# A hybrid decoder step on one core: another order for the opening's copies, table load, small loads and transposes

## The reference

```
h = rmsnorm(x, norm1_g);  z = h @ w_in             # 2824 columns
u, x_rg, g_rg, q, k, v, o, gi, gf = split(z)
y1, s5 state  = s5_mixer(u, ...)                   # diagonal complex state space model
y2, rg state  = rglru_mixer(x_rg, g_rg, ...)       # causal conv, two gates, recurrence
y3, ml state  = mlstm_mixer(q, k, v, gi, gf, o, ...)
x = x + concat(y1, y2, y3) @ w_out
x = x + moe(rmsnorm(x, norm2_g), ...)              # top 4 of 32 experts, clamped SwiGLU
y = rmsnorm(x, final_norm_g)

# s5_mixer, before its scan, from parameters alone:
step = exp(log_step); mag = exp(lam_re * step)
ab   = mag * (cos(lam_im * step) + i sin(lam_im * step))
z    = (ab - 1) / lam;   bb = z * b
```

## Time and profile before

| | |
|---|---|
| three runs | 1098.27, 1098.32, 1098.80 us; median 1098.32 |
| the profiled execution's own time | 1098.81 us |
| its span, first to last instruction | 1097.0 us (1.8 us lie around it) |
| PE busy | 1036.5 us, 94% |
| DVE, ACT, POOL busy | 316.1, 197.9, 95.3 us |
| HBM traffic over the span | 390 GB/s |
| mean granted TensorE clock | 0.993 |

### The profile page before, as it was taken

The page is one execution under the profiler, slowest core; times in us unless marked ns, Lnnn a source line. Parts: engine busy times, 40 slices in busy tenths (PEclk is TensorE's granted clock), DMA queues, the critical chain, the costliest instruction groups (busy, mean ns, idle before and its releaser), DMA issues.

```text
span 1097.0 us, 13183 instructions
## 1 busy us (share of the span) xinstructions
PE 1036.5 (94%) x5134; PEld 435.2 (40%) x5134; DVE 316.1 (29%) x640; ACT 197.9 (18%) x418; POOL 95.3 (9%) x177
## 2 busy tenths in 40 slices
PE   8999999999999999899889989999899989998997
PEld 5767745334333433343333323333324233433322
DVE  5889456312131212121202112121212121212023
ACT  5543615401110201011000201020102010100002
POOL 6899000000000000000000000000000000000000
PEclk9999999999999999999999999999999999999999
DMA  7533799999999999999999999999999999999995
GB/s 223 194 114 77 260 370 406 427 426 431 430 433 430 430 431 431 431 431 431 434 431 431 431 431 431 431 431 434 431 430 431 431 431 431 431 433 431 424 426 239
DMA packets 62051, 429.45 MB, mean 391 GB/s; under 512 B 12022, under 2 KB 25054, under 8 KB 33342
## 3 DMA queue, kind: packets, MB, share of 16 engines
q1 hardware_dynamic: 60868, 428.16, 93.5%
q10 hardware_dynamic: 1146, 0.79, 0.2%
HBM read 424.68 MB, written 3.67 MB: 390 GB/s over the span
## 4 chain that ended last, share of the span: by engine, by line
PE 55%; DMA 36%; DVE 5%; ACT 2%; issue 1%; SPq 1%; ACTq 0%; DVEq 0%
DMA ring_a<-in_exp_w_dram 27%; PE psum L2405 17%; PE psum L2440 14%; DMA ring_b<-in_exp_w_dram 8%; PE psum L2426 7%; PE psum L2327 3%; PE psum L2158 3%; PE psum L2350 2%; PE psum L1886 2%; PE psum L2449 1%; PE psum L2277 1%; PE psum L2283 1%; DVE rgb L1341 1%; SPq L449 1%; DMA xn<-in_x_prompt_dram 1%
## 5 line engine op out<-in xcount | busy, mean ns | idle before, releaser
L2405 PE MATMUL psum<-ring_a,xg 128*64 128x512 f32 x1200 | 341.8, 600 | 14.4 <-DMA ring_a<-in_exp_w_dram 14.4
L2440 PE MATMUL psum<-ring_a,aT 128*64 128x512 f32 x768 | 217.7, 596 | 8.5 <-DMA ring_a<-in_exp_w_dram 8.2
L2405 PEld LDWEIGHTS psum<-ring_a,xg 128*64 128x64 f32 x1200 | 102.9, 137 | 170.1 <-issue 166.0
L2405 PE MATMUL psum<-ring_b,xg 128*64 128x512 f32 x368 | 152.3, 598 | 7.8 <-DMA ring_a<-in_exp_w_dram 7.8
L1672 DVE TENSOR_TENSOR x<-x,psum 128x512 f32<-128x512 f32 x60 | 41.2, 687 | 367.7 <-PE psum L2350 367.7
L2426 PE MATMUL psum<-ring_a,xg 128*64 128x512 f32 x336 | 103.5, 608 | 14.2 <-DMA ring_b<-in_exp_w_dram 14.2
L2440 PEld LDWEIGHTS psum<-ring_a,aT 128*64 128x64 f32 x768 | 68.0, 137 | 110.2 <-issue 104.3
L2440 PE MATMUL psum<-ring_b,aT 128*64 128x512 f32 x256 | 104.0, 595 | 4.2 <-DMA ring_a<-in_exp_w_dram 2.6
L1760 DVE TENSOR_SCALAR acts<-psum 128x512 f32<-128x512 f32 x32 | 22.0, 688 | 223.3 <-PE psum L2426 207.8
L1045 ACT ACTIVATE acts<-acts 128x512 f32<-128x512 f32 x32 | 20.1, 627 | 296.5 <-DVE acts L1760 296.5
L2405 PEld LDWEIGHTS psum<-ring_b,xg 128*64 128x64 f32 x368 | 43.1, 136 | 75.5 <-issue 63.6
(11 more groups left out here) (508 smaller groups left out, 934.9 us busy)
## 6 DMA issues: line engine op xcount, KB each, us to landing
ring_a<-in_exp_w_dram SPq DMA_DIRECT2D x144, 2048.0 KB, 26.3
ring_b<-in_exp_w_dram SPq DMA_DIRECT2D x46, 2048.0 KB, 24.8
ring_a<-in_w_in_dram SPq DMA_DIRECT2D x4, 2048.0 KB, 8.5
ring_a<-in_w_out_dram SPq DMA_DIRECT2D x2, 2048.0 KB, 9.8
ring_a<-in_w_in_dram SPq DMA_DIRECT2D x3, 1024.0 KB, 5.9
ring_a<-in_state_ml_c_dram SPq DMA_DIRECT2D x4, 512.0 KB, 6.1
out_dram<-ring_a SPq DMA_DIRECT2D x4, 512.0 KB, 6.1
ring_b<-in_exp_w_dram SPq DMA_DIRECT2D x2, 1024.0 KB, 28.5
```

What stands on the lines that cost most here:

```text
L2405: m = M(psum[64 * x:64 * x + 64, bk, :], xg[:, k, u, 64 * x:64 * x + 64], w[x][:, 512 * bk:512 * bk + 512], start=False, stop=(k == KD - 1))
L2440: m = M(psum[64 * x:64 * x + 64, 4 + nn, :], aT[:, 2 * j + s, 64 * x:64 * x + 64], w[x][:, 1024 * s + 512 * nn:1024 * s + 512 * nn + 512], ...
```

## The change

1. VectorE copies five halves, in the order hT0, hT2, hT4, hT3, hT5; ScalarE copies only hT1.
2. TensorE's one wait for six copies is split: three left halves before u0, three right halves behind u0's fourth step. Of three warming matmuls between and behind the transposes one is left, behind the last.
3. `mag` waits for its own semaphore `mag_arg`, which L1252 raises (VectorE no longer waits for itself there), and ScalarE's wait for `angle_reduced` moves to just ahead of the first Sin, behind the other three functions.
4. On SyncE the five loads of the states' rows go ahead of the gate columns; `glw` goes behind w_in's second slab.
5. The `par` transposes move from between u1 and gp to behind the sixth step of xr0.
6. ScalarE's order of copies becomes u0, u1, gp, `bias_piece(0)`, par (was u0, `bias_piece(0)`, u1, par, gp).

```diff
 SyncE, if c == 1:
+                    for x, name in enumerate(("state_s5_re", "state_s5_im")):
+                        sp.dma_start(srow[64 * x:64 * x + 64, :], ...).then_inc(sem("par_loaded"), 16)
+                    sp.dma_start(prow[0:32, :], ...)       # state_ml_n
+                    sp.dma_start(prow[32:48, :], ...)      # state_rg_h
+                    sp.dma_start(prow[48:96, :], ...)      # state_rg_conv
                     sp.wait_ge(sem("wgate_zero"), 1)
                     sp.dma_start(wgate[:, :, 0:2 * H], w_in_cols(GI0, 2 * H)).then_inc(sem("wgate_loaded"), 16)
...
-                    (the same five loads)
                     sp.dma_start(gb[:], ...)
                     sp.dma_start(m0[:], ...)
+                if c == 2:
                     sp.dma_start(glw[:], ...)
-                if c == 2:
                     sp.wait_ge(*at("weights_zero", 1))
 ScalarE:
-            for i in range(2):
-                name = f"hT{2 * i + 1}"
-                await_fill(act, name)
-                for c in range(4):
-                    m = A(hT[:, 4 + c, 128 * i:128 * i + 128], bank(name)[...], ACT.Copy, scale=vec("norm1_g", 4 + c))
+            await_fill(act, "hT1")
+            for c in range(4):
+                m = A(hT[:, 4 + c, 0:128], bank("hT1")[...], ACT.Copy, scale=vec("norm1_g", 4 + c))
...
             A(sm[:, 1, :], vecs[:, NVEC:NVEC + J5], ACT.Exp).then_inc(says_now("step_ready"), 1)
-            act.wait_ge(*at("angle_reduced", 1))
+            act.wait_ge(sem("mag_arg"), 1)
             A(sm[:, 5, :], sm[:, 2, :], ACT.Exp).then_inc(says_now("mag_ready"), 1)
             A(rsm[:, 0:2], vec("rg_lambda"), ACT.Abs).then_inc(says_now("act_rg"), 1)
             act.wait_ge(*at("act_rg", 1))
             A(g_exp[:, 12:14], rsm[:, 0:2], ACT.Exp, scale=-1.0).then_inc(says_now("act_rg"), 1)
+            act.wait_ge(*at("angle_reduced", 1))
             A(sm[:, 6, :], sm[:, 9, :], ACT.Sin).then_inc(says_now("angle_ready"), 1)
...
             u_out(0)
+            u_out(1)
+            copy_out("gp", gate_parts, bank("gp")[:, 0:T])
             bias_piece(0)
-            u_out(1)
             copy_out("par", parT[:, 0:224], bank("par")[:, 0:224])
-            copy_out("gp", gate_parts, bank("gp")[:, 0:T])
 VectorE:
-            for k in (0, 2, 4, 5):
+            for k in (0, 2, 4, 3, 5):
...
-            dv(TT(sm[:, 2, :], lr, sm[:, 1, :], ALU.mult))
+            TT(sm[:, 2, :], lr, sm[:, 1, :], ALU.mult).then_inc(sem("mag_arg"), 1)
 TensorE:
             for k in range(2, 6):
                 turn_half(k)
-                if k == 3:
-                    keep_warm(1)
-            keep_warm(2)
-            for k in range(6):
-                b, f = FILLS[f"hT{k}"]
-                pe.wait_ge(drained[b], f + 1)
+            keep_warm(1)
+            def rows_turned(hf):
+                for i in range(len(TILES)):
+                    b, f = FILLS[f"hT{2 * i + hf}"]
+                    pe.wait_ge(drained[b], f + 1)
...
+            def state_rows(k):
+                if k == 5:
+                    pe.wait_ge(sem("par_loaded"), 16 * 5)
+                    await_bank(pe, "par")
+                    TR(bank("par")[:, 0:128], srow[:], ident[:])
+                    ends_fill(TR(bank("par")[:, 128:224], prow[0:96, :], ident[0:96, 0:96]), "par")
+            rows_turned(0)
             pe.wait_ge(sem("w_in0"), 16)
-            channels("u0", 0, 0)
+            channels("u0", 0, 0, lambda k: rows_turned(1) if k == 3 else None)
             channels("u1", 0, 128)
-            (the wait for par_loaded and the two transposes)
             pe.wait_ge(sem("wgate_loaded"), 16)
             gate_products()
             pe.wait_ge(sem("w_in0_right"), 16)
-            channels("xr0", 0, 256)
+            channels("xr0", 0, 256, state_rows)
```

More of the change, by code:

```diff
@@ L469, in _ @@
                 if c == 1:
+                    for x, name in enumerate(("state_s5_re", "state_s5_im")):
+                        sp.dma_start(srow[64 * x:64 * x + 64, :], a[name][0].rearrange("b (j g) p -> (b j) (g p)", g=2)).then_inc(sem("par_loaded"), 16)
+                    sp.dma_start(prow[0:32, :], a["state_ml_n"][0].rearrange("b h k -> (b h) k")).then_inc(sem("par_loaded"), 16)
+                    sp.dma_start(prow[32:48, :], a["state_rg_h"][0].rearrange("b (x n) -> (b x) n", x=2)).then_inc(sem("par_loaded"), 16)
+                    sp.dma_start(prow[48:96, :], a["state_rg_conv"][0].rearrange("b t (x n) -> (b t x) n", x=2)).then_inc(sem("par_loaded"), 16)
                     sp.wait_ge(sem("wgate_zero"), 1)
@@ L738, in _ @@
             act.wait_ge(drained[FILLS["vec"][0]], 1)
-            for i in range(2):
-                name = f"hT{2 * i + 1}"
-                await_fill(act, name)
-                for c in range(4):
-                    m = A(hT[:, 4 + c, 128 * i:128 * i + 128], bank(name)[:, 128 * c:128 * c + 128], ACT.Copy, scale=vec("norm1_g", 4 + c))
-                m.then_inc(drained[FILLS[name][0]], 1)
+            await_fill(act, "hT1")
+            for c in range(4):
+                m = A(hT[:, 4 + c, 0:128], bank("hT1")[:, 128 * c:128 * c + 128], ACT.Copy, scale=vec("norm1_g", 4 + c))
+            m.then_inc(drained[FILLS["hT1"][0]], 1)
             act.dma_start(bias_in[:, 0:512], a["exp_b1"][0].rearrange("e (q n) -> q e n", q=4)).then_inc(sem("bias_loaded"), 16)
```

## The result

The changed kernel took 1107.24 us in the median of four runs (1105.30 to 1109.58), the kernel before 1098.56 in the four beside them (1098.27 to 1098.89): a ratio of 1.008, 95% interval 1.006 to 1.010. It is slower by 8.7 us, where 0.5 us faster was forecast. The profiled execution is the slowest of the four, 1109.58 (span 1107.8).

What follows compares the result with a forecast made beforehand. The experts run at their weights' DMA rate, so the end follows the stream's start, set by TensorE, its own bound in the opening. 0.33 + 0.16 + 0.05 = 0.54 us earlier: median 1098.32 becomes 1097.8, range 1096.6 to 1099.1.

Steps and rivals of the forecast that it cites:

- Where the lead goes: At ScalarE's last i activation (48.95): of VectorE's 1.1 to 1.7 us lead only TensorE's 0.49 and 0.05 slack pass.
- one to one: The end shifts by exactly what TensorE gains or loses up to w_out's second half, issued at 128.36.
- Rival (c): Gain lost on VectorE between 58 and 66 us, 0.7 either side, or the starts give nothing: 1098.3; chance 0.12.
- Rival (d): Fewer warming matmuls drop TensorE to half clock in the opening, costing 1.6 us: 1099.4; chance 0.05.
- The start: Only three left halves stand ahead of u0, which starts at 13.12 or 13.13: gain 0.33 us, bounds 0 to 0.36.
- The Sin table ahead of its wait: ScalarE loads it from 14.6 to 15.9, without waiting for the angles; VectorE's L1269 at 16.65, 1.7 us earlier.
- The wait for B: VectorE at L1289 waits up to 0.6 us for B, loaded behind the states' rows, landing 19.9 to 20.4.
- The stream: Experts' weights on the DMA engines: rate stays 428 GB/s, only its start moves.
- The `par` transposes: Moved behind a step of xr0 they cost 0.22 instead of 0.38 us: gain 0.16, bounds 0 to 0.38.
- The end: w_out at 127.8 and the kernel's end both come 0.54 us earlier.
- The chances: Forecast 0.60; faster by over 0.2% (2.2 us) 0.05, within 0.91, slower 0.04.
- Four rivals: Whole lead passes (0.10), B lands late (0.11), gain lost on VectorE (0.12), half clock (0.05); 1096.7 to 1099.4.

Runs made afterwards that it cites:

- e16: e4 with GpSimd held by eleven small memsets behind its table, ahead of its waits for the scans: 1104.47 us, ratio 1.0038.
- e4: Kernel before with only the earlier sines (wait for the angles moved behind the three other functions): 1105.72 us, ratio 1.0045.
- e9: Whole changed kernel, one warming matmul, with only GpSimd held by eleven more memsets ahead of its table: 1099.90 us, ratio 1.0004.
- e5: e4 with GpSimd held by eleven extra small memsets at the start of its table: 1100.16 us, ratio 1.0024.
- e13: Changed kernel without its part 3 (sines as before), with three warming matmuls: 1099.06 us, ratio 0.9996.
- e8: Kernel before with eleven extra small memsets on VectorE ahead of scan 0, nothing else: 1104.23 us.
- e2: Kernel before with one warming matmul of three and nothing else changed: 1100.23 us, ratio 1.0018.
- e3: Changed kernel with parts 4 to 6 undone (SyncE's loads, par transposes, ScalarE's copies as before): 1103.96 us, ratio 1.0023.
- e7: e4 with VectorE's four products moved inside scans 4 to 7, behind their preparing steps: 1103.80 us, ratio 1.0043.
- e10: e6 with VectorE's four products moved into the scans: 1100.28 us, ratio 0.9994.
- e14: Changed kernel without its part 3 (sines as before), with its one warming matmul: 1101.75 us, ratio 1.0021.
- e6: Changed kernel with three warming matmuls and GpSimd held by eleven extra memsets at its table's start: 1099.56 us, ratio 1.0012.

## Why the prediction was wrong, point by point

**The step that failed is "Where the lead goes".** It followed a lead of 1.1 to 1.7 us as something that can only be passed on or be lost, and said of GpSimd's share of it that it "releases only one expert load that has time". The chain of waits cannot show what the lead did: an engine that runs earlier meets other instructions of another engine. GpSimd came to its table's steps of 512 elements (1.04 to 1.67 us each) while VectorE was in its convolution's short steps, each of which then waits for one to end. Which steps meet differs from one execution to the next (in e16's the second bias rest starts no later than before, and the second mixer's chain is hit). Shown by e4 (the loss without the rest), e9 (the rest without the loss) and e16 against e5 (it must be taken away ahead of the table's end).

The price "one to one" for TensorE's own gain failed as well. TensorE kept its 0.47 us up to the r matmuls in e13 and did not bring it to w_out.

**Rival (c) was the right place at the wrong size.** It saw L1459 take 0.90 for 16 elements and priced the meeting at 0.7 us either way, once, between 58 and 66 us. It is a queue of such meetings: 2.7 us from the second convolution to the second bias rest in the changed kernel alone. And the price was taken one to one to the end, where e8 shows 1.3 become 4.8, counted from the first copy: TensorE waits longer ahead of scans 2 to 5, may fall to half clock, scan 4 comes later, GpSimd's backlog is gone, and the four products cost 1.0 us more each. The rule on the shared ports was not weighed in the prediction, and it was the one that spoke against this change.

**Rival (d), the half clock, was thought unlikely and priced by itself.** It came, in the opening of the changed kernel and of e2, e3, e4, e7, e10 and e14, three of them with all warming matmuls (e4, e7, e10). There it costs little alone (e2's profiled span +1.2, e14's w_out 0.65 behind e13's). Its larger price is at the scans, from 75 us on, where the prediction did not look for it. In the changed kernel its stretch was the longest, u0 and u1 took 3.0 us more, and the new order of copies made VectorE wait for them, 1.6 and 1.5 us; the forecast bounded this at 0.5. I put the distance from e4's 1105.72 to 1107.24 down to this; that is argued, not shown, and no run here tells it apart in the medians.

**What held.** The start: from the first copy to u0 2.43 us before, 1.95 in the changed kernel and 1.96 in e13, a gain of 0.47 for the forecast's 0.33. The Sin table ahead of its wait, no drain to be seen; VectorE's next step at 16.16 for 16.65, 0.37 of which is the earlier first copy. The wait for B 0.7 us for "at most 0.6". The stream 428 GB/s. The `par` transposes gave nothing: from u0 to xr1 14.36 us before and 14.39 in e13, where 0.16 was forecast. The end only seems to have held: w_out is 0.55 earlier in e13 for 0.54, but that is luck. In that execution everything began 0.55 earlier, from the first copy on; at the r matmuls TensorE was 1.0 us ahead, at scan 0 VectorE 0.54, and the 0.47 that the change gave TensorE is not in it.

**The chances** gave 0.04 to slower. Four rivals, none more than 1.6 us from the kernel before, were nearly all priced one to one, in a stage whose own trace had a wait of 1.2 us in front of the scans and GpSimd busy for 51.28 of 61.94 us beside VectorE. What stays open: why in one execution the clock falls and in the next it does not (e9 fell behind a wait of 1.92 us, e6 did not behind the same, nor e16 behind 2.9), and with it what decides between the two groups of times in the kernel before; only one execution of each kernel has a trace.

## What to carry to other kernels

Before an engine is given an earlier start, lay its long instructions beside the short ones of the engine that shares its memory ports; a lead of 2 us on GpSimd cost 5 to 6 us here, and eleven idle memsets took it back. Price a delay by what stands behind it: a wait that can drop TensorE's clock, and a backlog that keeps two engines out of step, turn 1 us into 4. And where times fall in two groups, count the runs in each; a median of three says which group it met, not how often.

## What the runs showed of the hardware

A VectorE step with two SBUF inputs that starts behind a GpSimd instruction ends 0.04 to 0.06 us behind it when it is short (32 elements: 0.25 alone, 1.15 then) and later behind it when it is long (384 elements: 0.41 behind, with 0.56 to 0.85 us for the whole step elsewhere). A copy of 24 elements from SBUF to SBUF is held as well (0.18 and 1.12). It goes the other way too: GpSimd's L707, 1.40 or 1.41 us four times, took 1.60 or 1.61 the four times behind a held product. And half clock at the scans went with every traced execution of 1100.9 us or more, and with none below. Steps that have one operand in PSUM took 0.76 and 0.77 us for 576 elements in the scans of both kernels while GpSimd ran beside them.
